# Two fused transformer blocks on one core: gathers and scatters of routed tokens as split fp32r products, and the seams between stages reordered

## The reference, cut to what matters

```
first block, layer 0:  hs += rms(pool_mixer(rms(hs)));   hs += rms(swiglu(rms(hs)))      # d_ff 2816
                       kv_in = rms(hs); k = kv_in @ w_k + b_k; v = kv_in @ w_v + b_v
first block, layer 1:  hs += rms(attention(rms(hs) @ w_q + b_q, k, v) @ w_o + b_o)        # 16 heads of 64
                       hs += rms(swiglu(rms(hs)))
second block:          z = rms(h) @ w_in -> stick-breaking attention, mLSTM, gating -> h += y @ w_out
                       h += hierarchical_moe(rms(h))    # 32 experts, top 2 of a group of 8
                       h += sigmoid(rms(h) @ ple_gate) * (p @ ple_proj);  out = rms(h)
```

## Time and profile before

| | us |
|---|---|
| median of 3 runs (1142.43 to 1144.74) | 1144.29 |
| the profiled execution, whole | 1149.82 |
| its span, first to last instruction | 1148.1 |
| PE busy in it | 1046.3 (91%) |
| DVE busy | 523.0 (46%) |
| ACT busy | 402.8 (35%) |
| mean granted TensorE clock | 0.942 of 2.4 GHz |
| read from HBM | 210.35 MB, 184 GB/s over the span |

### The profile page before, as it was taken

How to read it: one execution, slowest core, us unless ns; L and a number is a source line. 1 busy time by engine, 2 the same in 40 slices (tenths; PEclk the granted TensorE clock), 3 DMA queues, 4 the chain that set the end, 5 groups by cost and what they waited for, 6 DMA issues and landing times.

```text
span 1148.1 us, 17320 instructions
## 1 busy us (share of the span) xinstructions
PE 1046.3 (91%) x7062; PEld 872.0 (76%) x7062; DVE 523.0 (46%) x964; ACT 402.8 (35%) x670; POOL 152.8 (13%) x216
## 2 busy tenths in 40 slices
PE   3799999997988799999969998798999999999966
PEld 2589999996868699999959997597465564655565
DVE  5645454337582555554363467744222322223154
ACT  3343333434373533333344466332111110111053
POOL 5333332101001243331110000001000000000000
PEclk8799999998999899999979999597999999999988
DMA  6325443425522245434642321174598898888401
GB/s 270 147 74 203 163 150 125 151 106 224 216 74 74 74 156 210 160 137 152 219 176 79 142 83 42 42 315 171 219 368 350 333 382 336 362 354 333 194 1 37
DMA packets 25646, 212.53 MB, mean 185 GB/s; under 512 B 2000, under 2 KB 5344, under 8 KB 5728
## 3 DMA queue, kind: packets, MB, share of 16 engines
q1 hardware_dynamic: 25568, 211.43, 48.0%
HBM read 210.35 MB, written 1.07 MB: 184 GB/s over the span
## 4 chain that ended last, share of the span: by engine, by line
PE 82%; DVE 6%; ACT 5%; issue 3%; POOL 3%; DMA 0%; POOLq 0%; DVEq 0%; ACTq 0%
PE ps L1124 46%; PE ps L1459 10%; PE ps L1444 5%; PE ps L1473 5%; PE ps L1481 5%; PE ps L1115 4%; ACT wh L606 2%; DVE wl L613 1%; DVE mix L1580 1%; POOL sq L479 1%; PE ps L1429 1%; PE ps L1161 1%; PE ps L1412 1%; ACT sq L585 1%; PE ps L1144 1%
## 5 line engine op out<-in xcount | busy, mean ns | idle before, releaser
L613 DVE TENSOR_TENSOR wl<-ring,wh 128x2048 fp32r<-128x2048 f32 (+2 forms) x110 | 223.2, 2033 | 223.2 <-ACT wh L606 223.2
L606 ACT ACTIVATE wh<-ring 128x2048 fp32r<-128x2048 f32 (+2 forms) x110 | 187.1, 1705 | 319.4 <-PE ps L1124 314.9
L1124 PE MATMUL ps<-xh,wh 128*128 128x256 f32 (+3 forms) x760 | 218.3, 287 | 8.9 <-DVE xl L2094 7.0
L1124 PE MATMUL ps<-xh,wl 128*128 128x256 f32 (+3 forms) x760 | 215.9, 284 | 0.0
L1124 PE MATMUL ps<-xl,wh 128*128 128x256 f32 (+3 forms) x760 | 215.7, 284 | 0.0
L1124 PEld LDWEIGHTS ps<-xh,wh 128*128 128x128 f32 (+3 forms) x760 | 142.6, 188 | 10.9 <-issue 9.2
L1124 PEld LDWEIGHTS ps<-xh,wl 128*128 128x128 f32 (+3 forms) x760 | 142.6, 188 | 0.2
L1124 PEld LDWEIGHTS ps<-xl,wh 128*128 128x128 f32 (+3 forms) x760 | 142.4, 187 | 0.0
L1459 PE MATMUL ps<-wring,xb 128*64 128x512 f32 x512 | 114.4, 600 | 2.2 <-issue 2.2
L1124 PE MATMUL ps<-acth,wh 128*128 128x272 f32 (+1 forms) x352 | 102.7, 292 | 3.8 <-POOL actl L494 3.8
L1124 PE MATMUL ps<-actl,wh 128*128 128x272 f32 (+1 forms) x352 | 101.5, 288 | 0.0
(11 more groups left out here) (327 smaller groups left out, 1571.2 us busy)
## 6 DMA issues: line engine op xcount, KB each, us to landing
wring<-in_w_eg SPq DMA_DIRECT2D x32, 2048.0 KB, 10.6
ring<-in_w_gu SPq DMA_DIRECT2D x22, 2048.0 KB, 8.2
wring<-in_w_ed SPq DMA_DIRECT2D x16, 2048.0 KB, 8.0
ring<-in_w_dn SPq DMA_DIRECT2D x16, 1408.0 KB, 6.0
ring<-in_w_z SPq DMA_DIRECT2D x7, 2048.0 KB, 8.0
ring<-in_w_out SPq DMA_DIRECT2D x4, 1152.0 KB, 5.1
ring<-in_w_q SPq DMA_DIRECT2D x2, 2048.0 KB, 14.0
ring<-in_w_o SPq DMA_DIRECT2D x2, 2048.0 KB, 10.5
```

The source lines that it names most:

```text
L606: act.activation(wh[:, j, 0:size], ring[:, slot, j * size:(j + 1) * size], ACT.Copy)\
L613: dve.tensor_tensor(wl[:, j, 0:size], ring[:, slot, j * size:(j + 1) * size], wh[:, j, 0:size].bitcast(F32), ALU.subtract).then_inc(sem("l ...
L1124: ins = mm(o, p, q, start=first and n == 0, stop=last and n == 2)
```

## The change

All the parts are in one diff:

- **Buffers.** Beside the two pairs there is a third pair, `third`, in the tails of ring slots 0 and 1. The first piece of w_gu0, w_q, w_gu1 and w_z goes there; all other pieces alternate between the two pairs. `buffer_free` waits for the piece that had the buffer before.
- **Loads.** w_q is loaded ahead of the bias table instead of behind it.
- **Norm seams.** DVE adds the even chunks, POOL the odd ones. Squares of the ffn entries go to `mix` and those ahead of q to `pre_squares`, so none waits for a free buffer. PE multiplies each high x as it comes by both first pieces, high and low (8 products a chunk), then sums the squares, then does the products with low x. The next piece is split ahead of 1/rms.
- **ffn to w_dn.** The first w_dn output waits for each activation row as it uses it, not for all of a half.
- **q, k, v.** x for q is hs times the gain; 1/rms is multiplied in when DVE takes a q output out (two operations instead of one). The q products come first, then k and v from hs times gain (POOL), again with 1/rms behind them; for v it is turned into a column by three transposes.
- **w_o.** A sum of squares follows two outputs later instead of one. Both first pieces of w_gu1 are split earlier.
- **Experts.** Tokens are split (`h2h`, `h2l`) and gathered with the fp32r one-hot `psel`, two teams wide (256 columns), half of the channels at a time: 16 products per call. The weight of a slot is multiplied into `he` by DVE; `combine` takes a pure one-hot `places` and y split in `yh`, `yl`: 16 products of 256 columns. PE's order in team b is gate_up(b), gather(b + 2), transposes(b), combine(b - 1), down(b); two gather calls stand ahead of the loop.

The core of the diff:

```diff
+        THIRD_FIRST = ("w_gu0", "w_q", "w_gu1", "w_z")
...
+                if name in THIRD_FIRST and p == 0:
+                    k = 2
+                else:
+                    k, turn_of = turn_of, 1 - turn_of
...
             stream("w_kv")
+            stream("w_q")
             sp_.wait_ge(sem("bias_out"), 16)
             sp_.wait_ge(sem("dn_psum"), 2 * KD)
...
-            for name in ("w_q", "w_o", "w_gu1", "w_dn1", "w_z", "w_out"):
+            for name in ("w_o", "w_gu1", "w_dn1", "w_z", "w_out"):
                 stream(name)
...
             for c in range(KD):
                 wait_hs(act, 1, c)
+                act.activation(xh[:, c, :], hs[:, c, N_META:], ACT.Copy, scale=V("mixpre1", c)).then_inc(sem("xh_ready"), 1)
                 square(act, "pre1", c, hs[:, c, :], T)
+            split_hi(act, "w_q", *halves("w_q", 1, PIECE)[0])
             rsqrt(act, chain, "pre1", D, T)
...
+            split_hi(act, "w_q", *halves("w_q", 1, PIECE)[1])
+            for x in halves("w_o", 0, PIECE):
+                split_hi(act, "w_o", *x)
...
+            def with_high(k):
+                pe.wait_ge(sem("xh_ready"), 2 * l * KD + k + 1)
+                for j in range(2):
+                    for part, w in enumerate(split_buffer(gu, 0, j)):
+                        for g in range(2):
+                            pe.matmul(ps[:, 2 * j + g, 0:n], w[:, k * 256 + g * P:k * 256 + g * P + P], xa[:, k, 0:n],
+                                      start=(k == 0 and part == 0), stop=False)
...
+            for k in range(KD):
+                with_high(k)
             for c in range(KD):
                 sum_squares(pre, c, n)
-            piece(0, 1)
-            with pe.Fori(1, NF // 2) as i:
+            with_low(0)
+            with_low(1)
+            piece(1, 0)
+            piece(1, 1)
+            with pe.Fori(2, NF // 2) as i:
...
-                    if c == 0:
-                        pe.wait_ge(sem("act_split"), l * NF + (j + 1) * (NF // 2))
...
+                        if c == 0:
+                            pe.wait_ge(sem("act_split"), l * NF + f + 1)
...
-                if c:
-                    sum_squares("mixpost1", c - 1, SEQ)
+                if c >= 2:
+                    sum_squares("mixpost1", c - 2, SEQ)
...
+            low = {1: ("w_q", halves("w_q", 1, PIECE)[1]), 4: ("w_o", halves("w_o", 0, PIECE)[0])}
+            for c in range(KD):
+                dve.wait_ge(sem("q_psum"), c + 1)
+                chain(dve.tensor_tensor(sq[:, c % 2, 0:SEQ], ps[:, c % 4, 0:SEQ], r[:, N_META:], ALU.mult))
+                dve.tensor_scalar(qT[:, c, :].rearrange("p (b q) -> p b q", q=P)[:, :, ::-1],
...
+                if c in low:
+                    split_lo(dve, low[c][0], *low[c][1])
...
+            for q in range(4):
+                dve.wait_ge(sem("h2h_ready"), q + 1)
+                part = slice(q % 2 * 512, (q % 2 + 1) * 512)
+                dve.tensor_tensor(h2l[:, q // 2, part], ps[:, 1 + q, :], h2h[:, q // 2, part].bitcast(F32), ALU.subtract)\
+                   .then_inc(sem("h2l_ready"), 1)
             dve.wait_ge(sem("rank_psum"), 1)
...
+            def pick(out, c, select):
+                at = slice(c * P, (c + 1) * P)
+                for k in range(NB):
+                    mm(out, h2h[:, k, at], select[:, k, :], start=(k == 0), stop=False)
+                    ins = mm(out, h2l[:, k, at], select[:, k, :], start=False, stop=(k == NB - 1))
+                return ins
...
                 for c in range(KD):
-                    ins = mm(ps[:, c // 2, c % 2 * SEQ:(c % 2 + 1) * SEQ], y[:, c * P:(c + 1) * P], weights,
+                    for y in parts:
+                        ins = mm(ps[:, c // 2, c % 2 * SEQ:(c % 2 + 1) * SEQ], y[:, c * P:(c + 1) * P], weights,
...
-                dve.tensor_tensor(he, sgate, ps[:, 4, FE:2 * FE], ALU.mult).then_inc(sem("he_ready"), 1)
+                dve.scalar_tensor_tensor(he, ps[:, 4, FE:2 * FE], small[:, 178:179], sgate, ALU.mult, ALU.mult)\
...
+                for i in range(2):
+                    dve.wait_ge(sem("y_ready"), 2 * b + i + 1)
+                    dve.tensor_tensor(yl[:, i * 512:(i + 1) * 512], ps[:, 6 + i, :], yh[:, i * 512:(i + 1) * 512].bitcast(F32),
```

More of the change, by code:

```diff
@@ L147, in bass_two_blocks @@
             wring = sb("wring", [P, 2 * CHUNKS, CHUNK], F32, turn)
+        with ExitStack() as turn:
+            third = []
+            for x in "hl":
+                sb(f"tile_{x}", [P, 2 * PIECE], F32, turn)
+                third.append(sb(f"third_{x}", [P, PIECE], F32R, turn))
         ring = sb("ring", [P, SLOTS, SLOT])
@@ L179, in bass_two_blocks @@
         with ExitStack() as turn:
[L180 to L181 removed]
+            h2h = sb("h2h", [P, NB, D], F32R, turn)
+            h2l = sb("h2l", [P, NB, D], F32R, turn)
         ctx.enter_context(nc.sbuf_tensor("x_room", [P, 18 * SEQ], F32))
@@ L239, in bass_two_blocks @@
         take = carve()
+        take(moe_room)
         wproj = take(2560)
         ppT = take(KD, SEQ)
-        ysb = [take(D) for _ in range(2)]
-        comb = [take(SEQ) for _ in range(3)]
-        psel = [take(NB, P) for _ in range(3)]
+        combx = take(SEQ)
         spread = take(4, SEQ)
@@ L249, in bass_two_blocks @@
         rscr = take(700)
-        second = take(SEQ)
+        weighed = take(SEQ)
         spare = take(SEQ)
@@ L325, in bass_two_blocks, with split_buffer, buffer_free @@
         SPLIT = [(name, 2 * n) for name, n, _ in STREAM if name not in UNSPLIT]
+        THIRD_FIRST = ("w_gu0", "w_q", "w_gu1", "w_z")
+        BUFFER, BEFORE = {}, {}
+        latest, turn_of = {}, 0
+        for name, n in SPLIT:
+            for p in range(n):
+                if name in THIRD_FIRST and p == 0:
+                    k = 2
+                else:
+                    k, turn_of = turn_of, 1 - turn_of
+                BUFFER[name, p], BEFORE[name, p] = k, latest.get(k)
+                latest[k] = (name, p)
+        def split_buffer(name, i, j):
+            p = i * 2 + j if type(i) is int else 4 + j
+            k = BUFFER[name, p]
+            return (third[0][:, :], third[1][:, :]) if k == 2 else (wh[:, k, :], wl[:, k, :])
+        def buffer_free(eng, name, i, j):
+            if type(i) is not int:
+                done, count = piece_done(name, i * 2 + (j - 2))
+            elif BEFORE[name, i * 2 + j] is None:
+                return
+            else:
+                done, count = piece_done(*BEFORE[name, i * 2 + j])
+            eng.wait_ge(sem(done), count)
         class Chain:
@@ L582, in square @@
             k = SQ0[name] + c
-            if k >= 4:
+            if k >= 4 and name != "pre1" and not name.startswith("ffnpre"):
                 act.wait_ge(sem("sq_used"), k - 3)
-            act.activation(sq[0:rows, k % 4, 0:n], src, ACT.Square, **kw).then_inc(sem("sq_ready"), 1)
+            act.activation(square_at(name, c)[0:rows, 0:n], src, ACT.Square, **kw).then_inc(sem("sq_ready"), 1)
         def rsqrt(act, chain, name, width, n):
@@ L597, in split_hi @@
                 act.wait_ge(sem(f"tile_ready{slot}"), rnd * 16 + 16)
-            if type(i) is not int or i > 0:
-                done, count = piece_done(name, i * 2 + (j - 2))
-                act.wait_ge(sem(done), count)
-            elif FIRST_PIECE[name]:
-                before, n = SPLIT[[x for x, _ in SPLIT].index(name) - 1]
-                done, count = piece_done(before, n + j - 2)
-                act.wait_ge(sem(done), count)
-            act.activation(wh[:, j, 0:size], ring[:, slot, j * size:(j + 1) * size], ACT.Copy)\
+            buffer_free(act, name, i, j)
+            high, _ = split_buffer(name, i, j)
+            act.activation(high[:, 0:size], ring[:, slot, j * size:(j + 1) * size], ACT.Copy)\
                .then_inc(sem("hi_done"), 1)
@@ L695, in body @@
                     silu(i * 2 + (j - 2), j)
-            ring_steps(act, gu, body, first=1)
+            silu(0, 0)
+            split_hi(act, gu, *halves(gu, 1, PIECE)[1])
+            silu(1, 1)
+            ring_steps(act, gu, body, first=2)
             for j in range(2):
@@ L1114, in sum_squares @@
                     pe.wait_ge(sem("sq_ready"), k + 1)
-                mm(ps[:, 6, 0:n], ones[0:rows, :], sq[0:rows, (k + 1 - chunks) % 4, 0:n], start=(c < chunks), stop=(c == last))\
+                mm(ps[:, 6, 0:n], ones[0:rows, :], square_at(name, c + 1 - chunks)[0:rows, 0:n], start=(c < chunks), stop=(c == last))\
                     .then_inc(sem("sq_used"), chunks)
@@ L1303, in _ @@
                 pe.wait_ge(sem("lo_done"), piece + 1)
+                high, low = split_buffer("w_z", i // 2, i % 2)
                 for q, (kind, b) in enumerate(outs):
@@ L1396, in _ @@
                 pe.wait_ge(sem("lo_done"), piece + 1)
+                high, low = split_buffer("w_out", c // 2, c % 2)
                 if c >= 4:
```

390 lines of the change are left out of this document (221 added, 169 removed).

## The result

The changed kernel takes 1092.85 us (median of 4 runs, 1091.42 to 1096.90) against 1144.51 of before: 0.955 of the time, 95% interval 0.952 to 0.958. The forecast was 1088.2 with a range of 1075 to 1104. The profiled execution has a span of 1091.4; the sum of the forecast had given 1092.0 for it, and only then taken off 5.5. One of the four runs of the second kernel of experiment 1 was in a slower state with a lower clock (1098.13 us) and is left out of its median.

What follows compares the result with a forecast made beforehand. PE's work and waits, 82% of the chain, were taken as the bound. Terms summed to -56.1 us: span 1148.1 to 1092.0, execution 1093.7, less 5.5 for the profiled execution's excess over the median: 1088.2, range 1075 to 1104.

Steps and rivals of the forecast that it cites:

- parts 4 and 6: 4: w_dn, wait for POOL and lost clock go, 7.2 us in two layers; 6: w_o outputs, waits go, 7.1 us.
- part 3: Ffn entries, first scaling to third piece: 5.1 us saved in layer 0, 6.2 in layer 1.
- the allowance for the low clock: Ffn entries: 3 us counted as lost to low clock while chunks trickle in, a choice between 0 and 6.
- Part 5: q, k and v: PE idles 18.8 us ahead of the scores behind w_o's load and split; net +16.4 us.
- the price of DVE's short operations: Wait ahead of the scores: q outputs, 1/rms columns, k and v operations priced at 0.48 us each.
- Part 1: Expert teams: gathers and combines fall to 1.92 us each, team period to 14.5; 51.4 us saved.
- Part 2: Way into the teams: +4.5 us, bounds 1 to 7, with 2.6 for the tokens' low pieces counted in full.
- The last step: Whole execution: 5.5 us taken off because the profiled execution of before lay above the median, 1093.7 to 1088.2.
- the z stretch: Layer 1's second w_dn output to the experts' p products: forecast 0; the z entry's -0.9 us was not carried.
- The rival on the DVE order: Teams: low y or a select ahead of `he` makes PE wait 0.8 us a team; +12, 1100 us, 12%.
- the one on the loads: Teams: loads do not go beyond 351 GB/s, so they hold up the teams; +26, 1114 us, 4%.

Runs made afterwards that it cites:

- experiment 1: Changed kernel with the splitting of w_o's first tile moved into the heads: ACT's and DVE's work, 1083.71 us; second kernel, DVE's low part only, 1083.50 us.
- experiments 5 and 6: 5: changed kernel, first w_dn output waiting for all rows of a half, 1099.79 us; 6: changed kernel, w_o sums of squares one output later, 1102.06 us.
- experiment 2: Three variants of the changed kernel: half of w_down's columns loaded from team 2 on, 1098.43 us; no overfull-expert branch, 1086.57; gathers inside teams done twice, 1119.26.
- 7: First kernel of experiment 1 with the overfull-expert branch taken once ahead of all teams instead of in each; 1075.55 us, 0.940 of before.
- experiment 8: The kernel before, unchanged, profiled a second time; 1143.64 us, span 1141.9.
- experiment 3: First kernel of experiment 1 with the four subtractions for the tokens' low part moved on DVE ahead of the routing wait for ACT; 1086.32 us, 0.947 of before.

## Why the prediction was right, and where it was not

**Parts 3, 4 and 6** hold by mechanism and size (-5.6, -7.7, -7.9, -6.8), and experiments 5 and 6 show for parts 4 and 6 that the edits named were the ones that paid. For part 3 no run takes its edits apart. Part 3 was short in layer 1 by 1.5, the allowance for the low clock being too large there. Against the second trace of before, parts 3 and 4 would each be 1.5 less in layer 1.

**Part 5** holds link by link: load 7.82 (8.0 forecast), high part 1.92, low part 2.29, and the rest, 308.7 to 313.57, 4.8 instead of 6.6, since an output's two operations overlap in part (0.42 and 0.35 us in 0.72). The idle time is 16.9 instead of 18.8; the stretch +13.3 instead of +16.4, of which 1.2 is less low clock ahead of v's end (254.69 to 296.65 is 42.0, 43.2 forecast). The step that was mis-sized is the price of DVE's short operations. Experiment 1 shows that the wait came from two engines' program order and that its work, put into the heads, still costs 2 to 5.

**Part 1 was too good by 7.3**, the largest miss. Gathers and combines did cost 1.92 each, as runs of products. DVE's order was no bound (PE waited for `he` in the last two teams alone, 2.1 us in all) and neither were the loads: they moved 408 to 420 GB/s, and PE waited for no chunk, even without the branch (experiment 2) and with a single one (7), where teams stayed 14.69 apart up to team 14. The sum missed two things: a team is 14.69 instead of 14.5, since the first two products of a gather start 0.22 us apart and those of a combine 0.20, where the rest are 0.12 apart (816.90 to 817.12 and 819.05 to 819.25), so each switch to this kind of product costs some 0.1 (14 x 0.19 = 2.7); and four pauses of 1.4 with 0.2 behind each, 6.4, of which experiments 2 and 7 show that the branch makes them, while that the short team lays them bare is likely and not shown alone. Against that stands 1.7 at the first gate_up (8.78 to 7.09), which experiment 8 shows to be the luck of the first trace of before. The "issue" of team 0 was in the trace of before (1.55 at 807.07); that the branch had a price and a cover of its own was not asked. It belongs among the things to look for behind a 17.89 us team.

**Part 2** came out as summed (+4.1), but by a wrong reason: the text says that the low parts of the tokens could not stand in DVE's idle time. They could, as experiment 3 shows: the first gather came 2.3 us sooner. That the whole gained by it is not shown.

**The last step**, taking off 5.5 because the profiled execution of before lay above its median, is where the whole time went wrong. The sum gave 1092.0 for the span and it was 1091.4. Experiment 8 shows where such an excess stands: 3.0 of its 6.2 us lie in the ffn entry and w_dn of layer 1, seams whose low clock the terms had already taken off, so that part was counted twice. The rest lies where the terms took nothing off for clock. The profiled execution of after lay at its median (1093.15 to 1092.85). By the medians, then, the change gained 51.7 and not the 56.1 of the sum, which was worked out from an execution of before above its median. That the sum met the span within 0.6 is luck in part, since the terms' own errors cancel: teams +7.3, q -3.1, ffn -2.0, the z stretch -1.7, w_dn -0.7, the rest under 0.5 each.

The rival on the DVE order (12%) did not come, nor did the one on the loads. The Trainium skill, "DMA: Bandwidth & Descriptors", section "Where 436 GB/s comes from", has about 358 GB/s a core as the bound for loads into SBUF. The trace disagrees, with 408 GB/s over 205 us. The range had been stretched for the DVE order and held the time without it.

## What to carry to other kernels

When a loop body gets shorter, list everything that it hid, the fetch of its own instructions with it: a branch that shows no cost in a body of 17.9 us cost 1.6 us in four of sixteen of 14.7. One branch ahead of the loop took these away and cost 3.4 us more once, so count both. And take a gain of a few us stretch by stretch: a shorter whole time can come from stretches that the edit never touched. When a load waits for an operation that has just been moved later, follow it through every engine that has work on the loaded tile in its program ahead of something urgent: ACT and DVE both had to let go before PE could run. And if single traces differ by the clock at seams, a correction from one trace to the median must not be added to terms that remove those same seams.

## What the runs showed of the hardware that was not expected

- Over 200 us with the queues never idle, loads moved 408 to 420 GB/s (without the branch 420), a little under the 423 of the earlier trace rows.
- A taken branch over code that is not run showed as 1.1 to 1.8 us of "issue" on PE, now and then 3.2 to 3.7. Behind pauses of 3.20, 3.51 and 3.67 us the granted clock was down for some 3 us (0.58, 0.59 and 0.50), behind 3.38 and 3.42 it stayed at 1.00, and behind the short ones the next gate_up took 7.09 instead of 6.87.
- The second gather ahead of the teams ran at a granted clock of 0.50 in three traces of the changed kernel and its variants and at 1.00 in the eight others. Only one of the three has an edit near it; what decides it no run shows.
